# HGRN recurrence and forget-gate attention run in shared periods, with projection strips as filler

## The chip, the cores and the metric

The kernel runs on one core of one Trainium2 chip. The metric is the device time of one execution in microseconds, the median over several runs. Lower is better. All times below are microseconds unless marked ns.

## The reference, cut to what matters

The model has two blocks over 512 tokens of width 1024. Only the mixing part of the first block is touched by the change:

```python
proj = rmsnorm(h) @ w_in            # fq fk fv (512 each), ff (8), gq gf gi gg (512 each)
# forget-gate attention, 8 heads of 64
log_f = log_sigmoid(ff + bias);  F = cumsum(log_f)
s = q k^T / 8 + F[t] - F[s], causal;  fox_out = softmax(s) @ v
# HGRN, 4 heads of 128
f = lb + (1 - lb) sigmoid(gf);  k = 1 - f;  S_t = diag(f_t) S_{t-1} + k_t i_t^T
rec = S_t^T silu(q_t);  rec = rmsnorm(rec) * silu(gg)
h = h + concat(fox_out, rec) @ w_out
# then cross attention on 256 memory rows: kv = rmsnorm(mem) @ w_xkv, q = rmsnorm(h) @ w_xq, ...
```

The rest (cross attention, a feed-forward of 4096, and a second block with a depthwise convolution, a state-space branch and another feed-forward) is the same before and after.

## The kernel before, in words

All activations lie with features on the 128 partitions and the 512 tokens along the free axis. Every projection is cut into **strips** of 128 output features: `STREAM` is the list of all strips in the order in which they are used, and `AT[name]` is the place of the first strip of a stage. Strip `j` uses weight buffers `wh[j % 4]` and `wl[j % 4]` and accumulates in PSUM bank `bank[j % 4]`. The weights are split in a high and a low part: SyncE's queue loads the raw strip (512 KB), ScalarE's `high(j)` (L773, L774) writes the rounded high part to `wh` and the negated high part to `wl`, and GpSimd's queue (L755) adds the raw weights onto `wl` with a second 512 KB transfer. A strip is 8 input tiles times three matmuls (L339 to L341: high times high, high times low, low times high), 24 in all. ScalarE refills a buffer with `step(j)` after strip `j` is done, so the weights of four strips can wait ahead of TensorE.

Every engine has its own instruction list, written out by hand, and executes it in order; semaphores tie them together. There are four PSUM banks for strips and four (`work[0..3]`) for all else; `work_bank(key, b)` makes TensorE wait until the last use of bank `b` was read.

After 12 HGRN strips (gf, gq, gi) the stretch of the change begins. It has these parts.

- **Four HGRN heads.** The head's attention inside a block of 128 tokens is built in 8 levels. For each level VectorE subtracts a reference from the running log-decay (`distance`, L1345), ScalarE takes exponentials of its two halves (`level_exps`, L858, L859), VectorE multiplies them onto k and q (L1417, L1418), TensorE forms four 128x128 products (L442) and VectorE copies them under a mask (`gather`, L1355, L1357). After the levels come the turn of k (`kt`), three block states (`hs`), the output (`ho`), and a matmul with a matrix of ones (`hn`, L466) that sums the squares of the output over the partitions and spreads the sum over all of them; ScalarE takes the root (`out_root`), and VectorE a 128x512 reciprocal (`out_rstd`, L1330) and the product with the gate (`out_norm`). In each head four strips stand as filler at fixed places: gg at level 2, and three of ff, fv, fq, fk as `FILL` says.
- **Memory norm.** The memory rows are scaled and split tile by tile, and the first memory strip runs along.
- **Eight attention heads of four query blocks, 32 units**, with the 16 memory strips (256 columns wide, `w=NMEM`), one for two units. A unit is: scores (L480) and a causal mask added in PSUM (L482), `fox_logits` on VectorE (L1466, adds the gate sums and takes the row maximum), `fox_exp` on ScalarE (L908), the reciprocal and the scaling on VectorE (L1485, L1487), a turn on TensorE (L401), a copy on ScalarE (L930), and the product with the values (L492). The gate sums of a head are brought onto all partitions by a matmul (`nf`, L473) and a copy (L903).
- Then the w_out strips, on the high and low tiles `XB` of both outputs.

## Time and profile before

| | |
|---|---|
| median of 3 runs | 2170.16 us (2169.98 to 2170.24) |
| profiled execution | 2169.9 us, its span from first to last instruction 2168.0 us |
| TensorE matmul busy in the span | 2003.7 us, 92% |
| ScalarE busy | 1123.8 us, 52% |
| VectorE busy | 1007.4 us, 46% |
| mean granted TensorE clock | 0.957 of full speed |

Busy time is the union of the instructions' durations. TensorE's matmuls are pipelined, so two neighbours overlap in their durations; the distance between two starts tells what one costs, not its duration. A granted clock of 1.00 is 2.4 GHz and one of 0.50 is 1.2 GHz.

### The profile page before, as it was taken

The page shows a single profiled execution, that of the slowest core. Times are in us where ns is not written, and L with a number is a line of the kernel's source. Part 1 is how long each engine was busy: PE and PEld are TensorE (multiplying, and loading weights), DVE is VectorE, ACT ScalarE, POOL GpSimd, SP SyncE. Part 2 cuts the span into 40 slices and gives each one's busy share as a digit, 9 for nine tenths or more (in the row PEclk, how much of TensorE's full clock was granted, in tenths as well). Part 3 has the DMA queues.
Part 4 walks back from the last instruction along what each step waited for, and adds up shares of the span by engine and source line. Part 5 has one row for each costly group of instructions (what it writes and reads, how often), then busy time and mean ns, then how long its engine had stood idle before and what let it go on. Part 6 is the DMA issues. An engine that isn't in the chain of part 4 may idle for free.

```text
span 2168.0 us, 26573 instructions
## 1 busy us (share of the span) xinstructions
PE 2003.7 (92%) x9386; PEld 1621.2 (75%) x9386; DVE 1007.4 (46%) x1634; ACT 1123.8 (52%) x1530; POOL 272.1 (13%) x318
## 2 busy tenths in 40 slices
PE   5888789889899999999999999998999989999996
PEld 4677656568578888887877787887877868888885
DVE  4246643223434223144788776667752334223134
ACT  6535544344444333344547888767846454334342
POOL 1100000001011111110111110110111101111110
PEclk9999878789999999998999999999999989999998
DMA  9834435348358888885877676785777867888884
GB/s 251 182 78 98 96 79 117 88 106 186 88 129 191 187 191 192 186 193 127 205 175 165 151 171 156 196 203 136 181 181 188 187 136 177 192 190 191 190 181 100
DMA packets 95624, 347.83 MB, mean 160 GB/s; under 512 B 10624, under 2 KB 10624, under 8 KB 94880
## 3 DMA queue, kind: packets, MB, share of 16 engines
q0 software_dynamic: 45216, 163.60, 41.6%
q1 hardware_dynamic: 46656, 170.19, 27.2%
q10 hardware_dynamic: 3648, 12.65, 1.7%
q8 instruction: 65, 1.06, 0.2%
q14 instruction: 39, 0.32, 0.0%
HBM read 342.14 MB, written 4.26 MB: 160 GB/s over the span
## 4 chain that ended last, share of the span: by engine, by line
PE 72%; DVE 11%; ACT 8%; DMA 4%; issue 3%; DVEq 2%; ACTq 1%; SPq 0%
PE bank L339 21%; PE bank L340 20%; PE bank L341 20%; DVE ssum L1636 4%; DMA arena<-scratch 2%; ACT wl L774 2%; ACT wh L773 2%; DMA wl<-in_weights 1%; PE work L401 1%; PE work L492 1%; PE work L442 1%; ACT arena L1047 1%; DVE xt L1673 1%; PE work L480 1%; PE work L549 1%
## 5 line engine op out<-in xcount | busy, mean ns | idle before, releaser
L773 ACT ACTIVATE wh<-raw 128x1024 fp32r<-128x1024 f32 x314 | 332.2, 1058 | 788.1 <-PE bank L341 731.8
L339 PE MATMUL bank<-XAh,wh 128*128 128x512 f32 (+1 forms) x1712 | 671.9, 392 | 31.2 <-DMA wl<-in_weights 25.6
L340 PE MATMUL bank<-XAl,wh 128*128 128x512 f32 (+1 forms) x1712 | 659.8, 385 | 0.0
L341 PE MATMUL bank<-XAh,wl 128*128 128x512 f32 (+1 forms) x1712 | 659.1, 385 | 0.0
L755 POOL DMA_DIRECT2D wl<-in_weights x314 | 271.9, 866 | 1860.8 <-ACT wl L774 1823.3
L339 PEld LDWEIGHTS bank<-XAh,wh 128*128 128x128 f32 x1712 | 328.7, 192 | 102.0 <-DMA wl<-in_weights 26.5
L341 PEld LDWEIGHTS bank<-XAh,wl 128*128 128x128 f32 x1712 | 327.7, 191 | 63.8
L340 PEld LDWEIGHTS bank<-XAl,wh 128*128 128x128 f32 x1712 | 328.8, 192 | 60.8 <-issue 0.7
L774 ACT ACTIVATE wl<-raw 128x1024 fp32r<-128x1024 f32 x314 | 327.4, 1043 | 0.0
L339 PE MATMUL bank<-XBh,wh 128*128 128x512 f32 x752 | 298.5, 397 | 3.2 <-DMA wl<-in_weights 3.2
L341 PE MATMUL bank<-XBh,wl 128*128 128x512 f32 x752 | 297.0, 395 | 0.0
L340 PE MATMUL bank<-XBl,wh 128*128 128x512 f32 x752 | 296.9, 395 | 0.0
L1636 DVE SCALAR_TENSOR_TENSOR ssum<-arena,vec,ssum 128x512 f32<-128x512 f32 x232 | 174.4, 752 | 21.6 <-issue 4.1
L339 PEld LDWEIGHTS bank<-XBh,wh 128*128 128x128 f32 x752 | 141.3, 188 | 38.6 <-DMA wl<-in_weights 4.0
L340 PEld LDWEIGHTS bank<-XBl,wh 128*128 128x128 f32 x752 | 141.3, 188 | 34.4 <-issue 0.7
L341 PEld LDWEIGHTS bank<-XBh,wl 128*128 128x128 f32 x752 | 141.2, 188 | 34.0
L1673 DVE SCALAR_TENSOR_TENSOR xt<-arena,vec,xt 128x512 f32<-128x512 f32 x96 | 72.2, 752 | 9.6 <-ACTq L1026 1.6
L1572 DVE TENSOR_TENSOR h<-h,bank 128x512 f32<-128x512 f32 x24 | 16.5, 689 | 111.7 <-PE bank L341 111.7
L442 PE MATMUL work<-early 128*128 128x128 f32 x224 | 40.5, 343 | 23.3 <-DVEq L1419 23.3
L1560 DVE SCALAR_TENSOR_TENSOR xt<-bank,rstd 128x512 f32<-128x512 f32 x32 | 22.1, 692 | 85.9 <-PE bank L341 85.6
L1224 DVE TENSOR_TENSOR ssum<-ssum,sq 128x512 f32<-128x512 f32 (+1 forms) x53 | 34.6, 653 | 49.0 <-ACT sq L1160 28.6
L442 PEld LDWEIGHTS work<-early 128*128 128x128 f32 x224 | 36.9, 248 | 26.8 <-issue 26.2
(301 smaller groups left out, 1819.7 us busy)
## 6 DMA issues: line engine op xcount, KB each, us to landing
raw<-in_weights SPq DMA_DIRECT2D x306, 512.0 KB, 6.9
wl<-in_weights POOLq DMA_DIRECT2D x306, 512.0 KB, 8.0
arena<-scratch ACTq DMA_DIRECT2D x16, 512.0 KB, 7.9
raw<-in_weights SPq DMA_DIRECT2D x8, 384.0 KB, 3.6
wl<-in_weights POOLq DMA_DIRECT2D x8, 384.0 KB, 5.7
h<-in_xT SPq DMA_DIRECT2D x2, 1024.0 KB, 6.7
spill<-cst ACTq DMA_DIRECT2D x8, 256.0 KB, 7.2
arena<-spill ACTq DMA_DIRECT2D x1, 2048.0 KB, 11.4
```

The costliest lines, as they stand in the source:

```text
L339: mm(bank[s][:, 0:w], hi, tile(X[0], k, w), start=(n == 0), stop=False)
L340: mm(bank[s][:, 0:w], hi, tile(X[1], k, w), start=False, stop=False)
L341: last = mm(bank[s][:, 0:w], lo, tile(X[0], k, w), start=False, stop=(n == len(kts) - 1))
L401: last = turn(w[:, c * P:(c + 1) * P], src[:, c * P:(c + 1) * P], ident)
L442: last = mm(w[:, c * P:(c + 1) * P], a[:, c * P:(c + 1) * P], b[:, c * P:(c + 1) * P], start=True, stop=True)
L755: pool.dma_start(wl[j % 4][:, 0:w.shape[1]], w, accum_op=ALU.add).then_inc(w_lo[j % 4], 16)
L773: act_(wh[j % 4][:, :], raw[j % 2][:, :], ACT.Copy)
L774: act_(wl[j % 4][:, :], raw[j % 2][:, :], ACT.Copy, scale=-1.0).then_inc(w_neg, 1)
L1224: TTop(ssum[:, 0:w], ssum[:, 0:w], sq[:, t % 2, 0:w], ALU.add)
L1560: leave(STT(xt[:, u % 2, :], ps[:, :], 0.0, rstd[:, :], ALU.max, ALU.mult), j)
L1636: STT(v[:, 0:S] if k == 0 else c, v[:, k:k + S], V("dw_w", t * CONV_K + k), c, ALU.mult, ALU.add)
L1673: STT(x, rawp[:, k % 2, tap:tap + S], V("sc_w", ct * SK + tap), x, ALU.mult, ALU.add)
```

## The change

It merges the HGRN heads and the attention heads in four **periods** of 12 steps and a fifth for the last attention heads.

- The strips ff, fq, fk, fv, gg form one list `"fox"` of 17, in the order fv0, ff, fq0, fk0, gg0, fv1, fq1, fk1, gg1, and so on. TensorE takes them by `fill`, one input tile (three matmuls) at a time: `FILLS` says how many tiles each step has. The first strip (`LEAD`) comes ahead of the periods.
- In period t, steps 0 to 7 are the levels of HGRN head t, step 8 the turn of k, step 9 the states, step 10 the output, step 11 the sums of squares. Beside them runs the attention of head pair t-1: of three steps, the first ends with the scores of a block for both heads, the logits follow in VectorE's next step, and the exponentials, the scaling and the turn in the third; the product with the values stands in the first step of the next three. Period 0 has no attention.
- Pair 3 runs in a fifth period, in which the 16 memory strips are the filler (`MEM_FILLS`, 128 tiles in 12 steps).
- Fox strips of period 3 stand in steps 0 to 7 alone. In steps 8 to 11 the memory tiles are scaled and split into the tiles `XA`, and the memory norm comes ahead of the first memory strip.
- The two heads of a pair have their scores on partitions 0 to 63 and 64 to 127, one after the other in two banks, and their outputs in one bank, alternating.
- The gate sums are written to DRAM once and read back for each pair by a transfer that spreads two rows over 128 partitions (`gates_out`, `gates_in`); the eight `nf` matmuls and their copies go.
- The output norm takes 128x4 sums per head (`head_sums`, `out_sums`), one root and one 128x16 reciprocal for all heads in the fifth period, and four small matmuls per head to spread the result (`head_spread`). The silu of gg is also taken once, there.
- The four scans are no longer all ahead of the first level: TensorE's first level waits on `hg_kq`, and scans 1 to 3 stand in VectorE's steps 1 to 3 of period 0.
- The first memory transfers move from SyncE's queue at the start to ScalarE's queue in period 3.

The core of the diff (TensorE's and ScalarE's lists, and the order of VectorE's):

```diff
-FILL = {(t, l): 1 + 3 * t + n for t in range(HG) for n, l in enumerate((4, "hs", "ho"))}
+STEPS = 12
+LEAD = KT
+FILLS = [[3, 3, 2] * 4, [3, 3, 2] * 4, [3, 3, 2] * 4, [4] * 8 + [0] * 4]
+MEM_FILLS = [10, 11, 11] * 4
+FV_TURN = [3, 5, 5, 5]
...
+            def fill(name, n, xn=None, w=S):
+
+                for _ in range(n):
+                    m, k = divmod(at_k[name], KT)
+                    at_k[name] += 1
+                    j = AT[name] + m
+                    b = j % 4
+                    if k == 0:
+                        pe.wait_ge(w_lo[b], 16 * (j // 4 + 1))
+                        pe.wait_ge(bank_free[b], j // 4)
...
+            def head_sums(t):
+
                 w = work_bank(("hn", t), 3)
                 wait_read(pe, ("ho", t))
-                mm(w[:, :], ones, sq[:, t % 2, :], start=True, stop=True).then_inc(wk_done[3], 1)
...
+            def fox_scores(p, i):
+                n = (i + 1) * P
+                w = [work_bank(("fs", p, i, hh), hh) for hh in range(2)]
+                for hh in range(2):
+                    rows = slice(FD * hh, FD * (hh + 1))
+                    mm(w[hh][:, 0:n], fq[rows, p * S + i * P:p * S + (i + 1) * P], fk[rows, p * S:p * S + n],
+                       start=True, stop=False)
...
+            for t in range(HG):
+                for s in range(STEPS):
+                    if s < LEVELS:
+                        level(t, s)
+                    elif s == 8:
+                        pe.wait_ge(sem("h_qk"), t + 1)
+                        turn_tile(("kt", t), 2, hZ[:, 0, :], 3)
+                    elif s == 9:
+                        head_states(t)
+                    elif s == 10:
+                        head_out(t)
+                    else:
+                        head_sums(t)
+                    n = FILLS[t][s]
+                    fill("fox", min(n, 1))
+                    fox_between(t - 1, s)
+                    if s == FV_TURN[t]:
+                        pe.wait_ge(sem("fv_raw"), t + 1)
+                        turn_tile(("fv", t), 2, xt[:, t % 2, :])
+                    fill("fox", n - min(n, 1))
+                    fox_at_end(t - 1, s)
...
+            def gates_out():
+
+                act.wait_ge(sem("f_neg"), 1)
+                act.dma_start(scratch[0:FH, :], fneg[0:FH, :]).then_inc(sem("f_out"), 16)
+
+            def gates_in(p):
+
+                if p == 0:
+                    act.wait_ge(sem("f_out"), 16)
+                else:
+                    act.wait_ge(sem("f_s"), 2 * TT * p)
+                act.dma_start(nfb[:, :, :], scratch[2 * p:2 * p + 2, :].partition_broadcast(P)).then_inc(sem("f_in"), 16)
...
+                    nearest(t, l)
                     gather(t, l - 1)
...
+                    if t and l % 3 == 1:
+                        fox_logits(t - 1, l // 3)
+                    elif t and l % 3 == 2:
+                        fox_normalise(t - 1, l // 3)
+                    if t == 0 and l < HG:
+                        scan(l)
+                    fox_strips(t, l)
+                    if t == 0 and l in (4, 6):
+                        fox_gates(l // 2 - 2)
```

In the fifth period ScalarE first takes the root of the 128x16 sums (step 0) and the four silus (step 1), and refills a weight buffer in the step after the one in which its strip was finished. In period 3 ScalarE scales memory tiles 0 to 2 in step 8 and 3 to 7 in step 11, VectorE its part of tiles 0 to 2 ahead of the states and of 3 to 7 behind the last logits.

## Rows read from the trace of the kernel before

**Rows 1.** Stretches: length, busy time of PE, PEld, DVE, ACT, POOL, clock, DMA share, GB/s.
```profile
154.00:199.00 45.00, 37.08 (x198) 31.56 (x196) 26.12 (x43) 23.40 (x36) 3.45 (x4) 0.92 0.42 93
...
312.00:472.00 160.00, 141.84 (x726) 101.84 (x726) 47.74 (x149) 64.95 (x133) 12.94 (x15) 0.82 0.46 100
96.00:472.00 376.00, 310.90 (x1538) 240.00 (x1537) 173.35 (x363) 177.96 (x310) 28.52 (x33) 0.84 0.43 95
...
500.00:520.00 20.00, 20.00 (x86) 15.91 (x85) 7.47 (x11) 11.17 (x14) 2.59 (x3) 1.00 0.89 186
```

**Rows 2.** Timeline of TensorE: start, length, line, idle before it and releaser.
```profile
106.89 2.05 PE L442 MATMUL work<-early,arena 128*128 128x128 f32 x8 [8.90 <-DVEq L1326]
...
117.16 1.95 PE L442 MATMUL work<-early 128*128 128x128 f32 x16
118.87 0.48 PE L339 MATMUL bank<-XAh,wh 128*128 128x512 f32 x1
...
131.57 2.05 PE L442 MATMUL work<-early 128*128 128x128 f32 x8 [5.20 <-DVEq L1419]
...
468.10 0.51 PE L339 MATMUL bank<-XBh,wh 128*128 128x512 f32 x1
```

**Rows 3.** Timeline of TensorE: attention, a memory strip, and pairs in the second block.
```profile
327.61 1.09 PE L492 MATMUL work<-arena 128*64 128x128 f32 x8
328.63 1.12 PE L480 MATMUL work<-arena 64*128 64x512 f32 x2
...
331.17 0.29 PE L341 MATMUL bank<-XAh,wl 128*128 128x256 f32 x1
331.29 0.28 PE L339 MATMUL bank<-XAh,wh 128*128 128x256 f32 x1
...
1242.89 0.42 PE L633 MATMUL work<-arena 128*64 128x128 f32 x4
1243.11 0.42 PE L637 MATMUL work<-arena 128*64 128x128 f32 x4
```

**Rows 4.** Timeline of VectorE: the scans, two successive levels, two successive memory tiles.
```profile
102.14 4.57 DVE L1325 TENSOR_TENSOR_SCAN arena<-cst,arena 128x512 f32<-128x512 f32 x4 [3.88 <-ACT arena L841]
...
218.61 0.69 DVE L1345 TENSOR_TENSOR early<-arena 128x512 f32<-128x512 f32 x1
...
221.54 0.68 DVE L1345 TENSOR_TENSOR early<-arena 128x512 f32<-128x512 f32 x1
...
295.18 0.48 DVE L1230 SCALAR_TENSOR_TENSOR XAl<-arena,vec,XAh 128x256 fp32r<-128x256 f32 x1 [0.17 <-issue]
...
296.17 0.48 DVE L1230 SCALAR_TENSOR_TENSOR XAl<-arena,vec,XAh 128x256 fp32r<-128x256 f32 x1 [0.17 <-issue]
```

**Rows 5.** Groups of VectorE by shape: a head, then the attention.
```profile
L1330 DVE RECIPROCAL std<-std 128x512 f32<-128x512 f32 x1 | 3.4, 3352 | 0.1
...
L1466 DVE CUSTOM_DVE_ANT_0 arena<-work,arena 128x512 f32<-128x512 f32 x7 | 4.8, 692 | 7.6 <-PE work L482 6.6 <-issue 0.7 <-PE work L401 0.2
...
L1487 DVE TENSOR_SCALAR arena<-arena,small 128x512 f32<-128x512 f32 x8 | 3.9, 486 | 0.7
```

**Rows 6.** Groups of ScalarE in the stretch of the change.
```profile
L773 ACT ACTIVATE wh<-raw 128x1024 fp32r<-128x1024 f32 x33 | 34.9, 1057 | 109.3 <-PE bank L341 109.3
...
L858 ACT ACT_TABLE_LOAD x8 | 10.3, 1283 | 0.1
...
L908 ACT ACTIVATE arena<-arena,small 128x512 f32<-128x512 f32 x8 | 5.8, 723 | 3.0 <-DVEq L1469 2.9
```

**Rows 7.** DMA issues of the whole program: count, size, median us to landing.
```profile
wl<-in_weights POOLq DMA_DIRECT2D x306, 512.0 KB, 8.0
arena<-scratch ACTq DMA_DIRECT2D x16, 512.0 KB, 7.9
```

**Rows 8.** Stretches of 2 us behind a wait in the attention (columns as in rows 1).
```profile
390.00:392.00 2.00, 1.13 (x3) 0.38 (x3) 0.00 (x0) 0.81 (x2) 0.86 (x1) 1.00 0.21 53
392.00:394.00 2.00, 1.97 (x8) 1.25 (x9) 0.92 (x4) 0.92 (x2) 0.00 (x0) 0.54 0.75 221
```

More of the change, by code:

```diff
@@ new lines, in _, with level @@
+            fill("fox", LEAD)
+            turn_values(HG - 1)
+            def level(t, l):
+                w = work_bank(("level", t, l), 2 + l % 2)
+                if l == 0:
+                    if t == 0:
+                        pe.wait_ge(sem("hg_kq"), 1)
+                    a, b = hkk[:, t * S:(t + 1) * S], hqq[:, t * S:(t + 1) * S]
+                else:
+                    pe.wait_ge(sem("h_z"), 7 * t + l)
+                    a = b = hZ[:, l % 2, :]
+                for c in range(TT):
+                    last = mm(w[:, c * P:(c + 1) * P], a[:, c * P:(c + 1) * P], b[:, c * P:(c + 1) * P],
+                              start=True, stop=True)
+                last.then_inc(wk_done[2 + l % 2], 1)
@@ new lines, in fox_turned, with fox_store, fox_first @@
+            def fox_turned(p, i):
+                n = (i + 1) * P
+                for hh in range(2):
+                    ps = wait_full(act, ("ft", p, i, hh))
+                    free(act_(fPT[:, hh, 0:n], ps[:, 0:n], ACT.Copy), ("ft", p, i, hh))
+            def fox_store(p, i):
+                ps = wait_full(act, ("fo", p, i))
+                free(act_(fq[:, p * S + i * P:p * S + (i + 1) * P], ps[:, 0:P], ACT.Copy), ("fo", p, i))
+                act.drain().then_inc(sem("f_o"), 1)
+            def fox_first(p, s):
+                if s % 3 == 0:
+                    if s and p >= 0:
+                        fox_turned(p, s // 3 - 1)
+                    elif s == 0 and p > 0:
+                        fox_turned(p - 1, TT - 1)
+                elif s % 3 == 2 and p >= 0:
+                    fox_exp(p, s // 3)
@@ new lines, in _ @@
+            level_exps(0, 1)
+            for t in range(HG):
+                for s in range(STEPS):
+                    if s == STEPS - 1:
+                        ps = wait_full(act, ("ho", t))
+                        act_(tile(hb, t), ps[:, :], ACT.Copy)
+                        if t == 0:
+                            act.wait_ge(sem("f_neg"), 1)
+                        free(act_(xt[:, t % 2, :], ps[:, :], ACT.Square), ("ho", t))
+                    fox_first(t - 1, s)
+                    if 1 <= s < LEVELS - 1:
+                        level_exps(t, s + 1)
+                    if t and s == 0:
+                        out_sums(t - 1)
+                    fox_stored(t - 1, s)
+                    if s == FV_TURN[t]:
+                        ps = wait_full(act, ("fv", t))
+                        free(act_(fv[:, :, t * P:(t + 1) * P], blocks(ps[:, :]), ACT.Copy), ("fv", t))
+                    if t == 0 and s == 5:
@@ L931, in _ @@
-            mem_turned(KT - 1)
+            for s in range(STEPS):
+                fox_first(HG - 1, s)
+                if s == 0:
+                    out_sums(HG - 1)
+                    root(NORM["mem"], dst=memrstd, w=NMEM)
+                    act.drain()
+                    act_(s_hn, s_hn, ACT.Sqrt, bias=eps_ap(EPS), scale=1.0 / P)
+                    act.drain().then_inc(sem("h_root"), 1)
+                    fox_refill(HG, 0)
+                fox_stored(HG - 1, s)
+                if s == 1:
+                    fox_refill(HG, 1)
+                    act.wait_ge(sem("gg_raw"), HG)
+                    for t in range(HG):
+                        act_(tile(hgg, t), tile(hgg, t), ACT.Silu).then_inc(sem("gg_s"), 1)
+                for m in MEM_DONE[s - 1]:
+                    step(AT["mem"] + m)
+                for m in MEM_DONE[s - 2] if s > 1 else []:
+                    if m >= KT:
+                        mem_turned(m - KT)
@@ L933, in _ @@
+            fox_turned(HG - 1, TT - 1)
+            fox_store(HG - 1, TT - 1)
+            for m in MEM_DONE[STEPS - 1]:
+                step(AT["mem"] + m)
+            for m in MEM_DONE[STEPS - 2] + MEM_DONE[STEPS - 1]:
+                mem_turned(m - KT)
             for n in range(KT):
@@ L1312, in fox_in @@
                     dve.drain().then_inc(sem("fv_raw"), 1)
+                elif name == "gg":
+                    leave(TTop(tile(hgg, t), ps[:, :], rstd[:, :], ALU.mult), j)
+                    dve.drain().then_inc(sem("gg_raw"), 1)
                 elif name == "fq":
@@ L1443, in _ @@
                 dve.drain()
-                fox_in(FILL[t, "hs"])
+                if t == 0:
+                    fox_gates(2)
+                if t:
+                    fox_normalise(t - 1, 2)
+                fox_strips(t, 8)
+                fox_strips(t, 9)
+                if t == HG - 1:
+                    for n in range(3):
+                        mem_low(n)
                 ps = wait_full(dve, ("hs", t))
```

452 lines of the change are left out of this document (222 added, 230 removed).

## The prediction, made blind

> **What bounds the kernel now.** I read the table of stretches first, then the waits and timelines inside the stretch of the change, then groups by shape. Outside the change TensorE runs dense: in 500 to 520 it is busy all the time at clock 1.00 with 86 matmuls, 0.233 us each, so a strip of 24 costs 5.6 us and an input tile of three 0.70 [rows 1]. From 96 to 472 it is different: busy 311 of 376 us, clock 0.84, DMA share 0.43 [rows 1]. Memory is no limit there; short waits and a low clock are. The w_out strips start at 468.1 [rows 2], so the stretch that can shrink is 96.0 to 468.1, 372.1 us long. The rest I leave as it is.
>
> A head takes 45 us (154 to 199), of which VectorE is busy 26 and ScalarE 23 [rows 1]. It can't be shorter now, because four strips and eight levels stand in fixed clumps: two levels follow each other at once, then TensorE waits 5.20 us for VectorE [rows 2]. What VectorE does meanwhile is in its rows: a 128x512 reciprocal of 3.35 us for the output norm [rows 5]. ScalarE loads an activation table of 1.28 us eight times to get back to the exponential, and as often to leave it [rows 6]. The 32 attention units and the memory strips take 160 us (312 to 472) at clock 0.82, where VectorE is busy 48 and ScalarE 65 [rows 1]: no engine is full, the order makes TensorE wait.
>
> **What the parts cost TensorE at full clock.** Two levels last from 117.16 to 118.87, 0.86 each [rows 2]. A memory tile is three matmuls of 0.12 [rows 3], 0.36, and a strip 2.9. Scores of 512 columns take 1.12 [rows 3]; over the four widths I take 2.6 per head, 5.2 per pair. Four products with the values take 1.02 [rows 3], 20 per pair 5.1 in the old order; the turns of a pair, at some 0.15, 3.0. In the second block the same shape with the two heads alternating between halves of the columns starts every 0.22 us for a group of four instructions, where the attention's eight need 1.02 [rows 3]: less than half. So the products of a pair should come to 2.2. The scores alternate between halves of the rows; no row shows what that gives, the bounds are 2.6 (full overlap) and 5.2 (none), and I take 4. A pair is then about 9. The Trainium skill says the same of both (TensorEngine Tiling, Theoretical Speedup: a small dimension of up to 64 gives up to 2x); by it the scores would be 2.6 and the sum 6 us shorter over four pairs. The trace agrees on the column side.
>
> One HGRN period is then, on TensorE: 32 tiles 22.4, 8 levels 6.9, the turn, states, output and value turn about 3.3 (some 15 products of 0.21), attention 9: 41.6. VectorE per level needs 2.93 with one eviction, 2.3 without [rows 4]. Per pair it adds the logits (0.69 at full width [rows 5], with its accumulator read and drain 0.9, 5.4 for all eight) and the scaling (0.49 [rows 5], 4.5 for all with the reciprocals). Less the reciprocal and norm (4.8) of the old head's 26.1, VectorE has 21.3 + 9.9 + 2.4 of drains = 34. ScalarE loses about 4 us of tables and roots and gains 8 exponentials (0.72 at full width [rows 6]), 8 copies and 4 stores, 28 in all. TensorE bounds the period, but in steps 0 to 7 only just: it has 26 there and VectorE 24.
>
> **The sum, part by part.**
> - *Start.* The wait of 8.90 ahead of the first level [rows 2] keeps its chain (logarithm, one scan, one distance, exponentials), but level 0 and three tiles move into it, and three of the scans (4.57 for four [rows 4]) leave. Level 1 starts at 106.9: 10.9 from 96.0.
> - *Period 0.* VectorE bounds it. Steps 1 to 7: 7 levels with eviction 20.5, three scans 3.4, gate work of 8-row instructions some 3; then steps 8 to 11 with TensorE's 12 of content and the last gate stage. 40. The old head from there to 154 had 45.
> - *Periods 1 and 2.* 41.6, plus 3 for TensorE and VectorE taking turns in steps 0 to 7, plus 2 to 4 for a transfer: `gates_in` is issued in ScalarE's step 11 behind copies and exponentials, and VectorE wants it a step and a half later, after TensorE's step 0 (5.5 us of content, in period 1 some 3.5). It lands after 7.9 [rows 7]. VectorE's next level stands behind the waiting logits, and TensorE's behind that. For a low clock behind such a wait, about 2. The sums are 49 and 47. That the eight `nf` matmuls are gone (each as wide as the 512-column scores, 1.12 [rows 3]) is in the 9 per pair already.
> - *Period 3.* Steps 0 to 7: 32 tiles 22.4, levels 6.9, attention 4, plus 5 for stalls and the gates: 38. Steps 8 to 11 have no filler. The chain there: masked copy, product, scaling 3.2, last eviction, tiles 0 to 2 at 0.99 each [rows 4], states 1.3, and on ScalarE the copies of the turned block only behind tile 2, so scores (2,3) at about 10, logits, exponentials 15, tiles 3 to 7 five more, the scaling between, sum ready at 21. Then the norm. 22. With TensorE at 1.2 GHz for the work in this hole and behind it, 5 more: 65.
> - *Fifth period.* TensorE's content is 46 + 9 + 6 = 61, but 16 strips are 16 MiB in 2 x 512 KB each. The dense stretch moves 186 GB/s at a DMA share of 0.89 [rows 1], 209 GB/s if full, or 5.0 us per strip and 20 per three steps. Four strips wait loaded. Strip 4 needs ScalarE's refill behind a root, two table loads of 1.28 and four silus (two passes of 1.06 [rows 6] start at about 8), plus 8.0 to landing [rows 7]: 18.5. The first three steps take 19, the others 20 each, the end 2, and the wait of strips 6, 7 and so on at a low clock 6: 87. The bounds are 61, no wait for weights at all, and 98: two refills in one step cost 4.2 on ScalarE and 8.0 to land, 12.2 per pair of strips, if nothing of it overlaps.
>
> Together 10.9 + 40 + 49 + 47 + 65 + 87 = 298.9 against 372.1: 73.2 less. The profiled execution had 2169.9, 0.26 under the median of the runs, so I expect 2096.7, 2097 rounded. The w_out stage begins with buffers less full than now; its first two strips may wait a microsecond each, which I leave in the range.
>
> **The rivals.**
> 1. *A cleaner run.* Stalls and gate waits hidden, full overlap of the scores, clock near 1.0: periods of 43, hole of 20, fifth 80. 10.9 + 38 + 43 + 42 + 58 + 80 = 272, the time 2070. For it: VectorE and ScalarE have a third of a period free. Against: steps 0 to 7 leave VectorE only 2 us.
> 2. *The clock stays ragged.* Now 16% of the clock is lost over 376 us [rows 1]: at two levels, 32% of the time at half, some 60 us extra. A wait of about 2 us was enough in 390 to 392, the next 2 us ran at 0.54 [rows 8]; my sum has 15 to 20 us for it. If the half-clock share stays 32%, the stretch loses 40 more where VectorE or the transfers don't hide it, say 30: 2125 to 2145, middle 2135. The Trainium skill warns of it (TensorE: Matmul & The Clock Gate, A second HAM failure mode: work cycling through PSUM banks with small idle pieces makes the clock oscillate). The trace has both: dips in 312 to 472 with narrow strips, few in the heads with wide ones (0.92 in 154 to 199 [rows 1]).
> 3. *The chain of a block isn't hidden* (slower). Scores, logits, two exponentials, scaling, turn, copies, product and store are 1.6 + 1.8 + 1.8 + 1.4 + 1.2 + 1.2 + 0.5 + 0.6 and seven handovers of 0.2, 11.5 us; a triple of levels alone is 9. Run in series by the in-order lists a triple is 20 instead of 12, which adds 8 x 4 x 4 = 128 and gives 2225. It decides from where a triple costs 4.6 more, 16.6: then 73 is used up. Against: each piece has its own step, and its successor stands behind filler of 1.4 to 2 us.
> 4. *It does nothing*: the waits move but stay as long, 2166 to 2174.
>
> **Chances.** The forecast (2080 to 2115) 0.55, cleaner 0.13, ragged clock 0.24, slower 0.06, nothing 0.02. The range from 2072 to 2140 leaves out about 0.2. A difference of under 0.2%, 4 us, I count as no change, since more than that is not to be told from the spread of such a measurement. Faster 0.92, same 0.02, slower 0.06.
>
> **What would show it.** Period starts (first level of a head) near 107, 147, 196 and 243; first memory strip near 308, w_out near 395. TensorE waits on VectorE in level 2 of periods 1 to 3 with the logits behind the transfer of the gates; none of the 5.20 kind [rows 2]. Products with the values at under 0.3 us a pair of heads, eight fewer 512-wide matmuls, VectorE's L1330 reciprocals gone, the activation table loads at L858 [rows 6] from 8 to 2 or 3. In the fifth period TensorE waits for `wl`, at a DMA share of 0.9. I am wrong if periods 1 and 2 last over 55, if the clock from 96 to 395 stays at 0.84, or if the time moves outside the stretch.

## The result, and the profile after

The changed kernel takes 2079.39 us (median of 4 runs, 2076.20 to 2081.94) against 2170.07 us (4 runs, 2165.83 to 2170.24) for the kernel before: ratio 0.958, 95% interval 0.9564 to 0.9597. The prediction was 2097, range 2072 to 2140. The time fell by 90.7 us where 73 were forecast. The profiled execution took 2081.2 us with a span of 2079.2 us, 88.7 less than the profiled execution of before.

First the stretches of the changed kernel, cut where a period begins; columns as in [rows 1]:

```profile
97.00:142.40 45.40, 36.54 (x196) 29.67 (x197) 32.23 (x54) 25.69 (x42) 3.45 (x4) 0.96 0.46 98
142.40:185.60 43.20, 42.53 (x265) 33.13 (x264) 29.31 (x69) 23.72 (x54) 3.46 (x4) 1.00 0.54 118
185.60:229.60 44.00, 43.55 (x282) 33.95 (x281) 28.61 (x68) 24.63 (x58) 3.45 (x4) 1.00 0.47 107
229.60:268.00 38.40, 37.43 (x233) 29.68 (x231) 24.57 (x57) 20.28 (x47) 3.45 (x4) 1.00 0.61 148
268.00:282.00 14.00, 6.64 (x43) 4.48 (x41) 6.72 (x19) 9.91 (x23) 0.86 (x1) 0.76 0.41 103
282.00:376.40 94.40, 73.47 (x542) 66.46 (x543) 33.91 (x78) 51.83 (x84) 13.38 (x16) 0.88 0.68 162
376.40:424.00 47.60, 47.60 (x197) 38.23 (x196) 13.01 (x20) 22.71 (x30) 6.51 (x8) 0.95 0.82 179
```

A period with a head and a pair of attention heads is now as long (43.2 and 44.0 us) as a head without attention was (45 [rows 1]), with TensorE busy for all but 0.7 and 0.5 us and the clock at 1.00. TensorE idles in two places: in the hole from 268 to 282, and in the fifth period, where its 73 busy us fill 94.

The cuts come from the timeline of TensorE: level 1 of head 0, the first levels of heads 1 to 3, the memory norm, the first memory strip, and the first w_out matmul with what stands ahead of it.

```profile
104.00 1.39 PE L461 MATMUL work<-early 128*128 128x128 f32 x8 [3.77 <-DVEq L1537]
...
142.39 1.05 PE L461 MATMUL work<-early,arena 128*128 128x128 f32 x8
...
185.55 1.06 PE L461 MATMUL work<-early,arena 128*128 128x128 f32 x8
...
229.55 1.06 PE L461 MATMUL work<-early,arena 128*128 128x128 f32 x8
...
285.84 2.05 PE L383 MATMUL work<-ssum,cst 128*128 128x512 f32 x2 [1.10 <-DVEq L1636]
286.90 1.20 PE L441 MATMUL bank<-XAh,wh 128*128 128x256 f32 x1
...
376.12 0.66 PE L410 MATMUL work<-cst,xt 128*128 128x128 f32 x2 [4.42 <-ACT arena L1025]
376.44 0.78 PE L348 MATMUL bank<-XBh,wh 128*128 128x512 f32 x1
```

So w_out starts at 376.4 and not at 468.1 [rows 2]: 91.7 us are gained ahead of it. About 2 are given back at once: from the first w_out matmul to the norm behind that stage it is 52.5 us (376.44 to 428.96), 50.4 before (468.10 to 518.47). TensorE has no wait in either stretch. What differs is the clock behind the wait of 4.42 us ahead of 376.12, which is a wait for ScalarE and not for weights: for 5 us it is 0.52.

```profile
376.44:381.44 5.00, 5.00 (x14) 3.97 (x13) 0.00 (x0) 0.38 (x1) 0.43 (x1) 0.52 0.94 236
```

### The profile page after: what moved, and what is told of

Read it like the earlier page. It is cut to its first block, busy times and chain, and to the rows that moved or that the text cites. A ratio compares the mean times of both kernels' runs of the same rounds, so it can differ in the third digit from the quotient of the medians.

```text
span 2079.2 us, 26609 instructions
## 1 busy us (share of the span) xinstructions
PE 1944.3 (94%) x9426; PEld 1586.0 (76%) x9426; DVE 989.6 (48%) x1615; ACT 1102.7 (53%) x1526; POOL 272.1 (13%) x318
## 3 DMA queue, kind: packets, MB, share of 16 engines
q0 software_dynamic: 45216, 163.60, 43.4%
q1 hardware_dynamic: 46512, 169.14, 28.8%
q8 instruction: 65, 1.06, 0.2%
## 4 chain that ended last, share of the span: by engine, by line
PE 66%; DVE 10%; ACT 9%; DMA 8%; issue 3%; ACTq 2%; DVEq 2%; SPq 0%
PE bank L348 18%; PE bank L350 18%; PE bank L349 18%; DMA arena<-scratch 4%; DVE ssum L1809 4%; DMA wl<-in_weights 3%; ACT wl L835 2%; PE bank L441 1%; ACT wh L834 1%; ACT arena L1168 1%; PE bank L443 1%; PE bank L442 1%; ACTq L1144 1%; ACTq L1152 1%; PE work L461 1%
## 5 line engine op out<-in xcount | busy, mean ns | idle before, releaser
L834 ACT ACTIVATE wh<-raw 128x1024 fp32r<-128x1024 f32 x314 | 331.9, 1057 | 701.4 <-PE bank L350 629.4
L348 PE MATMUL bank<-XAh,wh 128*128 128x512 f32 x1448 | 574.1, 397 | 27.2 <-DMA wl<-in_weights 23.2
L349 PE MATMUL bank<-XAl,wh 128*128 128x512 f32 x1448 | 567.2, 392 | 0.0
L350 PE MATMUL bank<-XAh,wl 128*128 128x512 f32 x1448 | 566.6, 391 | 0.0
L350 PEld LDWEIGHTS bank<-XAh,wl 128*128 128x128 f32 x1448 | 274.0, 189 | 58.2
L349 PEld LDWEIGHTS bank<-XAl,wh 128*128 128x128 f32 x1448 | 274.3, 189 | 56.3 <-issue 0.7
L441 PE MATMUL bank<-XAh,wh 128*128 128x512 f32 (+1 forms) x264 | 100.7, 382 | 13.8 <-DMA wl<-in_weights 13.8
L443 PE MATMUL bank<-XAh,wl 128*128 128x512 f32 (+1 forms) x264 | 92.3, 350 | 0.0
L442 PE MATMUL bank<-XAl,wh 128*128 128x512 f32 (+1 forms) x264 | 92.2, 349 | 0.0
```

What stands on the lines that cost most here:

```text
L348: mm(bank[s][:, 0:w], hi, tile(X[0], k, w), start=(n == 0), stop=False)
L349: mm(bank[s][:, 0:w], hi, tile(X[1], k, w), start=False, stop=False)
L350: last = mm(bank[s][:, 0:w], lo, tile(X[0], k, w), start=False, stop=(n == len(kts) - 1))
L441: mm(bank[b][:, 0:w], hi, tile(XA[0], k, w), start=(k == 0), stop=False)
L442: mm(bank[b][:, 0:w], hi, tile(XA[1], k, w), start=False, stop=False)
L443: last = mm(bank[b][:, 0:w], lo, tile(XA[0], k, w), start=False, stop=(k == KT - 1))
```

## The experiments

Each variant ran on the same chip as runs of the kernel before; I give its median and the ratio to them with its interval. The runs of a variant spread by 4 to 13 us. Behind the norm that follows w_out all kernels have the same code, and that part still took 1642 to 1657 us in the 14 profiles. So the lengths of periods in the profiles carry the conclusions where the times can't. There is one profile of each kernel. The changed kernel itself, the yardstick, stands at 0.958 (0.9564 to 0.9597).

| run | median us | ratio (95%) | period 1 | period 2 | level 0 of head 3 to norm | norm to w_out |
|---|---|---|---|---|---|---|
| changed kernel | 2079.39 | 0.958 (0.9564-0.9597) | 43.2 | 44.0 | 56.3 | 90.6 |
| before_light | 2147.33 | 0.990 (0.9876-0.9924) | | | | |
| recip_each | 2085.85 | 0.9616 (0.9593-0.9639) | 47.3 | 48.2 | 57.7 | 87.5 |
| tables_each | 2081.98 | 0.9597 (0.9581-0.9613) | 44.5 | 45.5 | 56.2 | 84.0 |
| logits_first | 2104.48 | 0.9701 (0.9683-0.9718) | 51.8 | 54.7 | 67.8 | 84.8 |
| heads_in_turn | 2085.76 | 0.960 (0.9569-0.9631) | 43.4 | 44.8 | 58.3 | 93.3 |
| gates_by_matmul | 2094.41 | 0.9652 (0.963-0.9673) | 45.3 | 47.9 | 60.0 | 92.7 |
| no_scaling | 2073.72 | 0.9563 (0.9537-0.9589) | 42.1 | 43.1 | 55.8 | 87.7 |
| two_of_three | 2066.50 | 0.9527 (0.9491-0.9563) | 40.7 | 41.3 | 51.9 | 88.6 |
| mem_lead | 2072.70 | 0.9563 (0.9542-0.9583) | 43.1 | 44.0 | 60.1 | 82.4 |
| refill_at_end | 2070.85 | 0.9548 (0.9522-0.9573) | 43.1 | 44.0 | 57.6 | 80.6 |
| half_low | 2068.04 | 0.9534 (0.9509-0.9559) | 43.1 | 44.0 | 56.2 | 83.5 |
| combined | 2065.72 | 0.9523 (0.9496-0.955) | 43.1 | 44.0 | 59.9 | 71.3 |

In mem_lead and combined the norm stands behind the first memory strip, so their last two columns are to be read as a sum (142.5 and 131.2, against 146.9).

### Is it the shared periods, or the lighter norm?

Kernel before, without the heavy parts of norm and gate:

```diff
-                free(act_(std[:, :], ps[:, :], ACT.Sqrt, bias=eps_ap(EPS), scale=1.0 / P), ("hn", t))
+                free(act_(std[:, :], ps[:, :], ACT.Copy), ("hn", t))
...
-                nc.vector.reciprocal(std[:, :], std[:, :])
...
-                        act_(tile(hgg, t), tile(hgg, t), ACT.Silu).then_inc(sem("gg_s"), 1)
+                        act_(tile(hgg, t), tile(hgg, t), ACT.Copy).then_inc(sem("gg_s"), 1)
```

> The kernel before, with its order untouched, but without the four wide reciprocals of the output norm and without the activation table switches for its root and for silu(gg): the root and the silu become copies and the reciprocal is left out, so the norm and the gate are not computed. Theory A (the gain comes from the shared periods, in which TensorE always has work): the 5.2 us waits of a head shrink, about 5 us per head, 20 in all, 2140 to 2155. Theory B (the gain comes from the lighter work on VectorE and ScalarE): at least half of the 90.7 us, 2125 or less.

2147.33 against 2167.72 on the same chip: 20 of some 90 us, in the range of theory A. But it is not 5 us a head. In the profiles the first w_out matmul starts 15.8 us earlier (452.27 against 468.10). From the first level of head 0 to the memory norm it is 185.2 us against 193.2, 2 us a head; the other 8.2 are gained from that norm to w_out (159.8 against 168.0 us, clock 0.84 against 0.80), where the only instructions made lighter are those of head 3's norm. Over 96 to 468 the clock rises from 0.84 [rows 1] to 0.87, but here that stretch has 16 us of w_out in it; up to w_out it is 0.86.

```profile
96.00:468.00 372.00, 317.13 (x1591) 246.12 (x1590) 162.22 (x363) 164.79 (x304) 30.22 (x35) 0.87 0.46 100
```

The other 70 come with the rest of the change: the shared periods, the heads side by side, and the gate sums without their matmuls. The parts are not independent, though, as the next two runs show.

```diff
+                    if t and l == 4:
+                        nc.vector.reciprocal(std[:, :], std[:, :])
+                        dve.drain()
                     if t and l % 3 == 1:
                         fox_logits(t - 1, l // 3)
```

> The changed kernel, with one 128x512 reciprocal of 3.35 us put back on VectorE in step 4 of periods 1 to 3 (on a tile of ones that nothing uses). Theory A: VectorE is busy 29 of 43 us in these periods and TensorE bounds them, so at most 2 us each, 2079 to 2086. Theory B: VectorE sets the pace of steps 0 to 7, 3.4 us each and more, 2089 to 2095.

```profile
142.80:190.05 47.25, 44.15 (x265) 34.39 (x264) 32.68 (x70) 23.86 (x54) 3.45 (x4) 0.96 0.50 108
190.05:238.25 48.20, 45.24 (x282) 35.13 (x280) 32.02 (x70) 24.83 (x58) 3.45 (x4) 0.96 0.45 100
```

This is the table of stretches, periods 1 and 2. They are 4.1 and 4.2 us longer for 3.35 of work, and the clock is 0.96. The time alone (2085.85) would have passed for theory A; the periods say B for this point: VectorE, busy 29 of 43 us, has nothing to spare in the levels. A mean busy share over the period hides that. Period 3, where four tiles stand in each of these steps and TensorE has more to do, grew by 1.4 only; that the tiles are the reason is argued, not tested.

```diff
+                    if t and s == 4:
+                        act_(s_tmp[:, 0:1], s_tmp[:, 1:2], ACT.Sqrt)
+                    if t and s == 6:
+                        act_(s_tmp[:, 0:1], s_tmp[:, 1:2], ACT.Silu)
```

> The changed kernel, with an activation of one column as Sqrt in step 4 and one as Silu in step 6 of periods 1 to 3, so four table loads of 1.28 us in each of them (nothing uses the result). Theory A: ScalarE is busy 24 of 43 us and a step ahead, 0 to 5 us in all, 2079 to 2084. Theory B: the exponentials of the next level come later and TensorE waits, 2.5 us for each switch, 15 in all, 2094.

1.3 and 1.5 us in periods 1 and 2, none in period 3: four table loads of 1.28 us are nearly hidden. The time is 2081.98. ScalarE has the slack that VectorE lacks.

### Who bounds a period: one load off each engine

```diff
-                for hh in range(2):
-                    TS(fS[:, hh, 0:n], fS[:, hh, 0:n], s_ri[:, hh:hh + 1], None, ALU.mult)
```

> The changed kernel without the scaling of the exponentials by the reciprocal of their sum (two instructions per block on VectorE, 3.1 us per pair by their mean lengths; the attention is then not normalised). The reciprocal put back on VectorE had lengthened periods 1 and 2 by 4.1 and 4.2 us. If VectorE bounds steps 0 to 7 by itself: each of periods 1 to 3 gets 1.5 to 2 us shorter (the part of the scaling that lies in those steps), 2070 to 2075. If TensorE bounds as well, so that VectorE is only level with it: under 1 us per period, 2076 to 2080.

1.1, 0.9 and 0.5 us off periods 1, 2 and 3: nearer to the second expectation (under 1 us each), though the time, 2073.72, is in the range of the first. TensorE shows where the rest went. It is now busy all the time, 42.09 of 42.09 us and 43.07 of 43.07, so its own content is the limit of these periods.

```diff
-                    mm(bank[b][:, 0:w], hi, tile(XA[1], k, w), start=False, stop=False)
+                    if w < S:
+                        mm(bank[b][:, 0:w], hi, tile(XA[1], k, w), start=False, stop=False)
```

> The changed kernel, with the second of the three matmuls of each input tile (high weights times low activations) left out of the 17 fox strips, so they are less exact. TensorE saves 0.23 us for each of 32 tiles, 7.4 per period. If TensorE bounds periods 1 and 2 over their length: 5 to 7 us shorter each, 2058 or less. If VectorE bounds steps 0 to 7: only steps 8 to 11 gain, 2 us each, 2072 to 2076.

```profile
141.20:181.90 40.70, 36.72 (x232) 27.37 (x231) 29.30 (x70) 23.30 (x54) 3.45 (x4) 0.98 0.50 117
```

TensorE has 5.8 us less (36.7 busy against 42.5) and the period is only 2.5 shorter; period 2 gives 2.7, period 3 4.4. The time, 2066.50, lies between the two expectations, and so do the periods. In periods 1 and 2 taking work from either engine returns less than half of it, and adding to VectorE costs all of it. The two are nearly level there, which is what the prediction's 26 against 24 us for the eight level steps said. In period 3, where TensorE's cut returned most, TensorE leads.

### The order in VectorE's step

```diff
+                    if t and l % 3 == 1:
+                        fox_logits(t - 1, l // 3)
                     nearest(t, l)
                     gather(t, l - 1)
-                    if t and l % 3 == 1:
-                        fox_logits(t - 1, l // 3)
-                    elif t and l % 3 == 2:
+                    if t and l % 3 == 2:
                         fox_normalise(t - 1, l // 3)
```

> The changed kernel, with the logits of a block first in VectorE's step instead of last (ahead of the products of the level). The scores end TensorE's step before, so VectorE then waits for them with the next level behind. If this order is what keeps TensorE fed: nine places (steps 1, 4 and 7 of periods 1 to 3) at 1 to 3 us each, 2088 to 2106. If VectorE's spare third covers it: 2079 to 2083.

2104.48, near the upper end of what the first case expected. The three periods grow by 8.6, 10.7 and 11.5 us, about 3.4 for each of the nine places:

```profile
141.20:193.00 51.80, 45.40 (x265) 35.99 (x264) 29.53 (x69) 23.68 (x54) 3.45 (x4) 0.93 0.45 100
193.00:247.60 54.60, 48.21 (x281) 37.67 (x280) 28.77 (x68) 24.75 (x58) 3.45 (x4) 0.91 0.38 86
```

VectorE's busy time is the same as in the changed kernel (29.5 and 28.8 us). Nothing was added; VectorE waits for scores that end TensorE's step, and the next level's factors are late. TensorE's waits over periods 1 and 2, as total, number and longest, were these in this run:

```profile
PE work L461 <- DVEq L1537: 12.8, 6, 2.4
```

and these in the changed kernel, from 142.4 to 268:

```profile
PE work L410 <- DVEq L1559: 1.5, 3, 1.0
PE work L461 <- DVEq L1537: 0.6, 2, 0.4
```

The falling clock (0.93, 0.91) adds to it.

### Gate sums, and the heads side by side

```diff
-                act.dma_start(nfb[:, :, :], scratch[2 * p:2 * p + 2, :].partition_broadcast(P)).then_inc(sem("f_in"), 16)
+                for hh in range(2):
+                    ps = wait_full(act, ("nf", p, hh))
+                    free(act_(nfb[:, hh, :], ps[:, :], ACT.Copy), ("nf", p, hh))
...
+            def nf(p):
+                if p == 0:
+                    pe.wait_ge(sem("f_neg"), 1)
+                for hh in range(2):
+                    w = work_bank(("nf", p, hh), hh)
+                    mm(w[:, :], ident[0:FH, 2 * p + hh:2 * p + hh + 1].broadcast_to([FH, P]), fneg[0:FH, :], start=True,
+                       stop=True).then_inc(wk_done[hh], 1)
```

> The changed kernel, with the gate sums brought onto all partitions as before, by one 512-wide matmul per head and a copy on ScalarE, in step 0 of the pair's period, in place of the transfers. If the price is TensorE's time: 1.1 us per head, 8.8 in all less what the fifth period hides, 6 to 8, plus a wait for the two copies ahead of the scores, 2085 to 2095. If the transfers made VectorE wait: no loss or a gain, 2072 to 2080.

2094.41, ratio 0.9652, its interval clear of the changed kernel's. Periods 1 to 3 grow by 2.2, 3.9 and 3.7 us. The two matmuls take 1.91 of it (191.03 to 192.94). Most of what periods 2 and 3 lose beyond that is the clock. Behind the matmuls it falls (0.57 over 192.94 to 196.94), and the next six strip matmuls start 0.43 us apart instead of 0.23:

```profile
191.03 1.98 PE L520 MATMUL work<-std,cst 8*128 8x512 f32 x4 [0.38 <-ACT arena L953]
192.94 0.62 PE L441 MATMUL bank<-XAh,wh 128*128 128x512 f32 x1
193.35 0.63 PE L442 MATMUL bank<-XAl,wh 128*128 128x512 f32 x1
```

Up to that point TensorE's longest wait in period 2 is the 0.38 in the first line. It went the same way in period 3 and in the fifth, but not in period 1, where no wait stood right ahead of the two matmuls and the clock stayed at 1.00. So in this kernel a wait of several microseconds was not needed for the clock to fall. What the matmuls and the short wait did each is not shown. The rival, that the transfers had made VectorE wait, falls. The timeline of the changed kernel agrees for the first pair. ScalarE issues the first of these transfers at 137.8 (the first start of its line in the view of the tensor `scratch`), the median to landing of all transfers from and to `scratch` is 7.8, which gives 145.6 as an estimate, and the first logits start at 146.28, where VectorE had waited 0.61 us, and for the scores:

```profile
142.59 0.69 DVE L1435 TENSOR_TENSOR arena<-bank,rstd 128x512 f32<-128x512 f32 x1 [6.38 <-PE bank L443]
...
146.28 0.29 DVE L1546 CUSTOM_DVE_ANT_0 arena<-work,arena 128x128 f32<-128x128 f32 x1 [0.61 <-PE work L512]
```

Next, products with the values one head after the other:

```diff
-                for c in range(i + 1):
-                    for hh in range(2):
+                for hh in range(2):
+                    for c in range(i + 1):
```

> The changed kernel, with the products of the values of one head of a pair after the other instead of alternating, so neighbours share their half of the columns. If alternating halves their price (0.11 us against 0.25), 20 products per pair cost 2.9 more, 12 in all where TensorE bounds (periods 1 to 3: 9 to 10; the fifth waits for weights), 2086 to 2092. If the alternation gives nothing: 2079.

The timelines of TensorE in period 2, first the changed kernel, then this one, with the eight products of the widest block and the strip that follows:

```profile
187.23 1.09 PE L527 MATMUL work<-arena 128*64 128x128 f32 x16
188.26 0.50 PE L441 MATMUL bank<-XAh,wh 128*128 128x512 f32 x1
```

```profile
187.68 1.58 PE L527 MATMUL work<-arena 128*64 128x128 f32 x16
189.19 0.50 PE L441 MATMUL bank<-XAh,wh 128*128 128x512 f32 x1
```

1.03 us against 1.51. The periods grow by 0.2, 0.8 and 2.0. The ratio 0.960 (0.9569 to 0.9631) can't be told from 0.958. The expectation of 12 us was wrong. Why, the other widths tell. These are the distances from the start of a group of products to the start of what follows it, at full clock:

| products per head | 1 | 2 | 3 | 4 |
|---|---|---|---|---|
| kernel before, one head | 0.37 | 0.58 | 0.80 | 1.02 |
| changed kernel, both heads, alternating | 0.37 | 0.59 | 0.81 | 1.03 |
| heads_in_turn, both heads | 0.37 | 0.60 | 1.07 | 1.51 |

One head alone costs 0.22 us per product and 0.15 once per group. Two heads alternating cost the same as one, so the second is free at every width. Over the four widths a pair takes 2.80 us instead of 5.54. In turn it takes 3.55, not 5.54, since the products at the border of the two heads still overlap: two of each head take 0.60, where four of one head take 1.02 [rows 3]. That the heads use different halves of the columns is worth 2.7 us a pair, of which 0.8 hang on the strict alternation. The run expected all of it to hang on that.

```profile
164.82 0.66 PE L527 MATMUL work<-arena 128*64 128x128 f32 x8
165.42 0.50 PE L441 MATMUL bank<-XAh,wh 128*128 128x512 f32 x1
```

The scores gave more than expected. The pair's widest scores take 1.06 us for both heads:

```profile
221.54 1.13 PE L509 MATMUL work<-arena 64*128 64x512 f32 x4
222.60 0.28 PE L512 MATMUL work<-neg_bf,ident_bf 128*128 128x128 bf16 x2
```

One head alone took 1.05 in the kernel before (328.63 to 329.68; its duration in [rows 3] is 1.12), so the second head is free when it lies on the other half of the rows too. Over the four widths a pair costs 2.95.

### The fifth period

The view is ScalarE's timeline in the changed kernel. L834 begins a refill.

```profile
327.81 1.06 ACT L834 ACTIVATE wh<-raw 128x1024 fp32r<-128x1024 f32 x1 [0.17 <-issue]
...
329.72 1.04 ACT L834 ACTIVATE wh<-raw 128x1024 fp32r<-128x1024 f32 x1
...
334.02 1.06 ACT L834 ACTIVATE wh<-raw 128x1024 fp32r<-128x1024 f32 x1 [2.31 <-DMA raw<-in_weights]
...
340.96 1.06 ACT L834 ACTIVATE wh<-raw 128x1024 fp32r<-128x1024 f32 x1 [3.73 <-DMA raw<-in_weights]
...
350.37 1.06 ACT L834 ACTIVATE wh<-raw 128x1024 fp32r<-128x1024 f32 x1 [0.17 <-issue]
```

Two refills stand together, the next two wait for their raw weights, then none starts for 9 us; the cycle of 22.6 us repeats. The DMA share is 1.01 in one stretch of ten and 0.68 over the period:

```profile
310.00:320.00 10.00, 6.89 (x46) 6.68 (x45) 4.54 (x12) 3.23 (x8) 1.73 (x2) 0.83 1.01 249
```

So the queues are full in bursts. TensorE's waits in this period, as total, number and longest, are mostly for weights; the second largest is for ScalarE's copies of the memory values (L1025), the last of which stands behind two refills (371.8 to 375.6) in ScalarE's order:

```profile
PE bank L441 <- DMA wl<-in_weights: 13.8, 6, 4.9
PE work L410 <- ACT arena L1025: 4.7, 2, 4.4
```

The edit refills in the step in which a strip ended:

```diff
-                for m in MEM_DONE[s - 1]:
+                for m in MEM_DONE[s - 1][1:]:
                     step(AT["mem"] + m)
                 for m in MEM_DONE[s - 2] if s > 1 else []:
                     if m >= KT:
                         mem_turned(m - KT)
+                for m in MEM_DONE[s][:1]:
+                    step(AT["mem"] + m)
...
-            for m in MEM_DONE[STEPS - 1]:
+            for m in MEM_DONE[STEPS - 1][1:]:
```

> The changed kernel, with ScalarE's refill of a weight buffer at the end of the step in which its strip ended (the first of two in steps 2, 5, 8 and 11) instead of the step after. In the trace of the fifth period two refills stand together at the start of each third step, then ScalarE waits up to 4.8 us for raw weights, with a DMA share of 0.68. Theory C (the bunched refills leave the queues empty between them): 2 to 4 us for each of the four triples, 2064 to 2072. Theory D (the transfers as such bound it, as the prediction had it): no more than 2 us, 2077 to 2080.

The stretch from norm to w_out in this run, and after it the changed kernel from half a microsecond behind its norm to w_out:

```profile
286.40:367.00 80.60, 69.45 (x535) 62.53 (x535) 30.15 (x70) 48.87 (x77) 13.45 (x16) 0.92 0.84 196
```

```profile
286.40:376.40 90.00, 70.94 (x534) 64.39 (x533) 30.77 (x70) 48.46 (x77) 13.38 (x16) 0.90 0.71 168
```

80.6 us, with the DMA share up from 0.71 to 0.84. TensorE's waits for weights are down from 13.8 to 2.7, those for the copies (one refill fewer stands ahead of the last) from 4.7 to 2.3:

```profile
PE bank L441 <- DMA wl<-in_weights: 2.7, 2, 1.4
PE work L410 <- ACT arena L1025: 2.3, 1, 2.3
```

The five profiles of kernels that leave this stretch's code alone (changed kernel, recip_each, tables_each, logits_first, two_of_three) have 84.0 to 90.6, 87.1 in the mean, so this is below all of them. Their waits for weights are 10.3 to 13.8. This is theory C: the stretch was not at the limit of the transfers. The ratio alone (0.9548, 0.9522 to 0.9573) would not say so, as its interval overlaps with that of the changed kernel. Ahead of it, 1.3 us more were spent from head 3 to the norm than in the changed kernel, which this edit does not touch.

The run that cuts bytes:

```diff
-                pool.dma_start(wl[j % 4][:, 0:w.shape[1]], w, accum_op=ALU.add).then_inc(w_lo[j % 4], 16)
+                n = w.shape[1] // 2 if AT["mem"] <= j < AT["mem"] + 2 * KT else w.shape[1]
+                pool.dma_start(wl[j % 4][:, 0:n], w[:, 0:n], accum_op=ALU.add).then_inc(w_lo[j % 4], 16)
```

> The changed kernel, with the second transfer of the 16 memory strips (the raw weights added onto the low part) cut to half of the columns, so the low part of the other half is wrong. Their bytes fall by a quarter. If the bytes bound the fifth period: its 90 us fall by 12 to 20, 2060 to 2067. If the bunched order of the refills does: 3 to 8 us less, 2071 to 2076, since the chain of raw transfer, split and low transfer keeps its steps.

A quarter fewer bytes gives 83.5 us, a smaller gain than a better order gives with all of them. The drop of 7 from 90.6 is in the range that the bunched order expected, but 83.5 is only half a microsecond below what the five profiles with unchanged code reach, and the time, 2068.04, lies between the two expectations. TensorE's waits for weights say more: 7.9 us, below the 10.3 to 13.8 and above the 2.7. Bytes count in the bursts, but don't bound the period.

```diff
-MEM_FILLS = [10, 11, 11] * 4
+MEM_FILLS = [10] * 12
...
-MEM_DONE = strips_done(MEM_FILLS)
+MEM_DONE = strips_done(MEM_FILLS, LEAD)
...
+            fill("mem", LEAD, tiles_from("mem"), NMEM)
             norm(NORM["mem"])
```

> The changed kernel, with the first memory strip ahead of the memory norm, taking its tiles as they come (as the kernel before did), and 10 tiles in each of the 12 steps of the fifth period. If the hole between the last filler of period 3 and the first memory strip costs its length: 3 us earlier plus 1 of better spread, 2073 to 2077. If the fifth period is bound by the arrival of weights: a strip done earlier only lets its refill start earlier, 3 to 6 us all the same; a result of 2079 or more would say that neither counts.

From head 3 to w_out 142.5 us instead of 146.9. That is no clear gain, since tables_each, which only adds table loads there, has 140.1. The time, 2072.70, is 7 us lower, but its interval overlaps with that of the changed kernel. Then all together, with the silus of gg behind the first refills:

```diff
+                if s == 0:
+                    step(AT["mem"])
-                for m in MEM_DONE[s - 1]:
+                for m in MEM_DONE[s - 1][1:]:
+                    step(AT["mem"] + m)
...
+                if s == 1:
+                    act.wait_ge(sem("gg_raw"), HG)
+                    for t in range(HG):
+                        act_(tile(hgg, t), tile(hgg, t), ACT.Silu).then_inc(sem("gg_s"), 1)
+                for m in MEM_DONE[s][:1]:
+                    step(AT["mem"] + m)
```

> The changed kernel with three edits of ScalarE's and TensorE's order in the fifth period together: the first memory strip ahead of the norm with 10 tiles per step, each refill at the end of the step in which its strip ended, and the four silus behind the first refills. If the edits add up (7 and 9 us measured alone, against runs of 2079): 2060 to 2066. If both only remove the same wait for weights, and the w_out strips then wait for theirs: 2068 to 2071.

2065.72 us (5 runs, 2060.83 to 2070.26), ratio 0.9523 (0.9496 to 0.955), the interval wholly below that of the changed kernel. It is the best version that I have. Head 3 to w_out takes 131.2 us, 15.7 less than in the changed kernel. That is far outside the spread, and TensorE's waits for weights are down to 1.7 us. It is what the edits would give if they added up (4.4 and 8.7 measured alone), but mem_lead's share isn't sure and the move of the silus was not run alone. The w_out stage keeps its 52.8 us.

## Why the prediction was right, point by point

- **What bounded the kernel, and where the gain would come from.** Right. The stretch went from 372.1 to 280.4 us (96.0 to 376.4), the w_out stage lost 2.1, and all else is within 1 us. That heavy instructions were the smaller part of the loss is shown by before_light: 20 us without them, 90 with the whole change. TensorE's waits over periods 1 and 2 came to about 1 us, where two old heads had 8 and 9 (154.6 to 199.9 and 199.9 to 246.5). Some of the gain is work that TensorE no longer has: per pair 2.7 us of products, 2.95 of scores (5.9 for two heads apart) and 2.1 of `nf` matmuls, by estimate 31 us over four pairs.
- **Start and period 0.** Forecast 50.9 from 96.0, measured 46.4. Level 1 started at 104.0 and not at 106.9, with one scan ahead of it instead of four. That is 2.9 of the 4.5; period 0 itself was 1.6 shorter than forecast. Which of their terms were too large is open.
- **Periods 1 and 2.** Forecast 49 and 47, measured 43.2 and 44.0. The terms as written (41.6, 3, 2 to 4, and 2) add up to 48.6 to 50.6, so the 47 was 1.6 below its own sum. The content of 41.6 was right to 2 us; the 3 for taking turns and the 2 to 4 for the gate transfer were not paid. By the estimate above the first transfer lands just before its logits. The 2 for the clock weren't paid either: with no longer waits, the clock stayed at 1.00. That the two engines are level in the level steps was right, and is why recip_each cost more than its own length.
- **Scores and products.** Scores of a pair 2.95 instead of 4; the full overlap was the right end of the bounds. Products 2.8 instead of 2.2. The cause was right, and so was the price of 0.11 per product taken from the second block; what the term left out is the 0.15 that each of the four groups costs once, 0.6 in all. The rule of the Trainium skill (TensorEngine Tiling, Theoretical Speedup: up to 2x for a dimension of up to 64) holds here to the full 2x on both sides: 1.06 against 1.05 on the rows, 1.03 against 1.02 on the columns, two heads against one.
- **Period 3 and its hole.** Forecast 65, measured 57.4 to the first memory strip. TensorE's last tile there starts at 264.6, the norm stands at 285.8: 21 for a forecast of 22, and the low clock did reign in it (0.50 in 282 to 288). But steps 0 to 7 took 35 for 38, without the 5 us of stalls, and of the 5 put on top for the low clock little was paid: TensorE's slow work in the hole lay beside the chain of the others.

```profile
282.00:288.00 6.00, 4.13 (x12) 2.73 (x13) 3.15 (x8) 4.03 (x9) 0.00 (x0) 0.50 0.09 34
```

- **Fifth period.** Forecast 87, measured 89.5 (286.9 to 376.4), but for the wrong reason, so the agreement is luck. I had it bound by the rate of transfers at 209 GB/s, with a DMA share of 0.9; the share is 0.71, a stretch above shows 249 GB/s in a burst, and refill_at_end shows that the order of the refills sets its length. The wait of 4.4 us for ScalarE's copy at its end was not in the sum at all.
- **The w_out stage.** I had allowed its first two strips a wait of a microsecond each. The 2.1 us were lost, but to the low clock behind the wait of 4.42; no strip waited for weights.
- **The rivals.** The clean run (2070) was nearer than the forecast, except in the fifth period; 2079.39 lies in the range, just below the 2080 to 2115 that got the 0.55. The ragged clock did not come over periods 1 and 2; from 96.0 to w_out it was 0.94, with 0.90 left in the fifth period, against 0.84 before. For this rival the prediction put the fall in [rows 8] down to the wait of 2 us. One of the 8-row `nf` matmuls stands between that wait and the fall (390.87 to 391.92), and gates_by_matmul has such a fall with a wait of only 0.38, so the wait may not be all of the cause. That the change took these matmuls out may be part of why the clock got better; no run tests that on the kernel before. The hidden chain held, and logits_first shows how little separates it from being exposed: one order inside VectorE's step is worth 25 us.

The sum was 18.4 us too high over the stretch: 4.5, 5.8, 3.0 and 7.6 too much, 2.5 too little. What was mis-sized in the shared periods is the allowance for stalls and clock, which I put on every period though the waits behind both were what the change removed. The errors go one way except in the fifth period, where a wrong reason gave nearly the right length.

Open: why the fifth period varies from 84 to 91 us in profiles whose code is the same there; how much of the gain is owed to each part of the new order, since no run has the shared periods alone; and whether the hole could be filled, since its tiles are written over the input of the filler. The last wasn't tried.

## What to carry to other kernels

When two phases each leave TensorE with short waits, interleave them step by step with filler of one input tile, and put what answers to TensorE's end of step last in the next step of the other engine; here that order was worth 25 us, the lighter instructions in the old order 20. Judge an engine's slack by the steps in which it is chained to another, not by its busy share over the period: 29 of 43 us busy was no slack at all, and to find that out, add a known load and see whether the period grows by it. Spread the refills of weight buffers as the strips end; here two at once left the queues full for 10 us and partly idle for the rest of each cycle, and TensorE waited 13.8 us for weights instead of 2.7. Put two products on different halves of the rows or columns side by side: here the second was free.

## What the runs showed of the hardware

- Two 64-row fp32 scores of 512 columns on the two halves of the rows, issued back to back, took 1.06 us together, as long as one. Two sets of 64-column fp32 products alternating between the halves of the columns took 1.03 us for eight, as long as four of one head in the kernel before (1.02). One set after the other took 1.51.
- The clock stayed at 1.00 from 142 to 268 in which TensorE changed between strips, small fp32 products and turns, with no wait over 1.0 us; it was 0.50 behind the waits of the hole. With six waits of up to 2.4 us put into periods 1 and 2 by logits_first it was 0.93 and 0.91. In gates_by_matmul it fell to half behind two 8-row matmuls of 512 columns (1.91 us) with no longer wait than 0.38 before it in that period, in periods 2 and 3, and not in period 1.
- Transfers reached 249 GB/s over 10 us at a DMA share of 1.01, against the 209 that the prediction had worked out from the dense stretch.
- Two one-column activations that need other tables, and the ways back, four loads of 1.28 us in all, made periods 1 and 2 longer by 1.3 and 1.5 us, on a ScalarE that is busy 24 of 43 us, and period 3 not at all.
